# First layer's queries, keys and values in three passes of two-part weight tiles, the recurrence products spread among them, and a second buffer for the state matrices

## The chip, the core and the metric

The kernel runs on one core of a Trainium2 chip. TensorE (PE) multiplies, VectorE (DVE) and ScalarE (ACT) do the elementwise work, GpSimd (POOL) and SyncE (SP) mostly issue transfers; all share an on-chip memory (SBUF), TensorE writes into PSUM banks, and inputs, outputs and intermediate stores lie in the chip's HBM. The metric is the device time of one execution in microseconds; of several runs the median counts.

## What is computed

One sequence of 256 tokens of width 2048 goes through two layers of attention and then through a block with a state-space mixer and an MLP. All of it is float32. Cut to what the change touches:

```python
def first_block(...):
    c_act = jax.nn.silu(c)
    for l in range(DEPTH):                                   # 2 layers
        mod = c_act @ w_mod[l] + b_mod[l]
        shift, scale, gate = jnp.split(mod, 3, axis=-1)
        h = x * (1.0 + scale[:, None]) + shift[:, None]
        y = diff_attention(h, ...) if l < N_A else forgetting_attention(h, ...)
        x = layer_norm(DN_ALPHA * x + gate[:, None] * y, ln_g[l], ln_b[l])
    return x

def diff_attention(h, w_in, w_out, lq1, lk1, lq2, lk2, subln_g, layer_idx):
    proj = h @ w_in                                          # 2048 x 8192
    q, k, v, g = jnp.split(proj, 4, axis=-1)
    ...
    return (rms_norm(o, subln_g) * (1.0 - lam_init) * silu(g)) @ w_out

def s5_scan(u, lam_bar, b_bar, s0, reverse):                 # second block
    bu = jnp.einsum('btgh,gph->btgp', u, b_bar)
    ...                                                      # s_t = lam_bar * s_(t-1) + bu_t
def s5_mixer(h_ctx, h_lat, ...):                             # both directions
    st_ctx = s5_scan(uc_ctx, lam_bar, b_bar, s0, reverse)    # 256 context tokens
    st_lat = s5_scan(uc_lat, lam_bar, b_bar, s_ctx_final, reverse)
    y_lat = y_lat + jnp.einsum('btgp,ghp->btgh', st_lat, c_mat).real
```

The second block's context half (`ctx_2`, the matrices b, c and the eigenvalues) doesn't depend on the first block.

## The kernel before

**Engines.** Each engine has a program written by hand, and semaphores tie them together: a `wait_ge` for one filled or emptied buffer. Weights come in loads of 1 MB that SP issues in one fixed order into a ring of six slots; the load for a slot waits till what stood in it is used up (`spent`). `tables` walks through the same order and hands out slots and PSUM banks, so every program lists the work in the same sequence: 56 "mods" (one mod is a group of 512 columns of the modulation parameters: four loads, 16 matmuls with the column of c as operand, and before them four small `sel` sums of the mod before), the first layer's 16 projection panels of 512 columns (four loads each, handled in halves 0 to 31: queries are halves 0 to 7, keys 8 to 15, values 16 to 23, gates 24 to 31), the context work of the second block, then the 20 + 4 panels around the second layer, the GLU and the MLP ("steps"). The tables `MOD_AT_*` say after which step of a loop a mod stands.

**Two ways to multiply.** The steps run in three passes: ACT copies a weight tile rounded to fp32r as its high part, DVE subtracts (raw - high) for the low part, in place in the ring slot, and PE adds high x high, high x low and low x high. The first layer's panels run in plain float32 instead, straight from the ring: `dense_T` (128x256 results, queries and keys) and `dense_N` (128x512, values and gates), with `hT`, the turned and modulated x, as the other operand. ACT and DVE copy the result of a half to a staging buffer (three of them in MSB, later four more), and POOL's queue stores it (`proj_out`).

**The stages, in order.** (1) Parameters 0 to 7, x turned (`turn_in`), and the 16 turns of b and c by matmuls with the identity (`to_state`). (2) The loop over 16 chunks of the recurrence's kernel: DVE makes the operand `cl` of a chunk with one `cmul` (six operations of 128x1152, then the corner copies of the chunk's product), POOL copies four corner blocks to BBD and stores `cl` to HBM, and PE does a projection half, at every other chunk a mod, and the product `kk` (16 matmuls from BBD). (3) The broadcast columns for the context (`acol`, made by DVE after the lambda vectors of the first layer, which POOL loads at that place), the rows of ctx turned into tables with 32 small matmuls for each `u` product, through copies of 32 rows and DMAs back into SBUF (`arena<-arena`), among them projection halves 18 to 21 and mods 16, 17. (4) The state matrices: in each of 16 chunks `bl` (DVE's `cmul`, six operations of 128x1024), 16 turns by the identity, ACT's four copies into the one buffer MSB (`vmat`), the product `vc` (32 matmuls of 64x32 from MSB) and a store of MSB to `m_state` in HBM, after which ACT may overwrite MSB; halves 22 to 31 stand before chunks 0 to 9 and mods 18 to 24 after seven of them. (5) SP loads the stored projections p0 to p3, and the differential attention runs in 20 steps with mods 25 to 30 at steps 1, 4, ..., 16. (6) The steps of both layers, the GLU and the MLP, with mods 31 to 50 at steps 0 to 19 and 51 to 55 in the second attention.

**Names in the rows.** `arena` is the big SBUF buffer, in which operands, `hT` and the tables lie; `ring`, `in_lo`, `in_hi`, `hid_lo`, `hid_hi`, `MSB`, `BBD`, `cpad` (the column of c), `mod_rows` are SBUF buffers of their own, `bank` is PSUM, `ident` the identity, `sel` the selector of the sums. L1847 is `mm` and L1850 `tr` on PE, L1192, L1196, L1200 and L1204 are DVE's helpers, L777 and L824 ACT's copy and rounding copy.

## Time and profile before

| | us |
|---|---|
| runs shown (3) | median 3030.43, 3026.02 to 3031.03 |
| the profiled execution | 3018.68 |
| its span from first to last instruction | 3016.9 |
| PE busy in it | 2666.4 (88%) |
| DVE busy | 1406.7 (47%) |
| ACT busy | 1005.5 (33%) |
| POOL busy | 155.2 (5%) |
| moved by DMA | 699.74 MB, 232 GB/s in the mean |

The profile is one execution; its time is 0.39% below the median of the runs. A busy share holds for the whole span, and the stages have different limits, so what one engine waits for is read stage by stage. By stage of the list above the profile stands like this: parameters and x to 126 us, turns of b and c to about 147, the projections with the recurrence products to 474.7, the context's tables to 570, the state matrices to 841, the loads and the first attention to 939. The rows in a section below use a few forms. A row of a timeline begins with its start and its duration in us; "x32" is the count of instructions in it, and what stands in brackets is the time that the engine was idle before it and what ended the wait. In a group of rows the numbers after the bar are busy time, mean ns of one, and idle time before them.

### The profile page before, as it was taken

The page shows a single profiled execution, that of the slowest core. Times are in us where ns is not written, and L with a number is a line of the kernel's source. Part 1 is how long each engine was busy: PE and PEld are TensorE (multiplying, and loading weights), DVE is VectorE, ACT ScalarE, POOL GpSimd, SP SyncE. Part 2 cuts the span into 40 slices and gives each one's busy share as a digit, 9 for nine tenths or more (in the row PEclk, how much of TensorE's full clock was granted, in tenths as well). Part 3 has the DMA queues.
Part 4 walks back from the last instruction along what each step waited for, and adds up shares of the span by engine and source line. Part 5 has one row for each costly group of instructions (what it writes and reads, how often), then busy time and mean ns, then how long its engine had stood idle before and what let it go on. Part 6 is the DMA issues. An engine that isn't in the chain of part 4 may idle for free.

```text
span 3016.9 us, 40552 instructions
## 1 busy us (share of the span) xinstructions
PE 2666.4 (88%) x17321; PEld 2087.0 (69%) x17321; DVE 1406.7 (47%) x2074; ACT 1005.5 (33%) x1569; POOL 155.2 (5%) x239
## 2 busy tenths in 40 slices
PE   3899996999767959989999986788969999999996
PEld 0488863445535758769875766567859899898995
DVE  4445441243535766433333453725455545555554
ACT  0200002111224323333332434724454444344443
POOL 2012341000000000000000001000000000000000
PEclk9799998999778979989997795798989999999998
DMA  9868997678597848867886544994534565656552
GB/s 309 310 230 315 346 380 242 193 271 277 205 362 282 313 170 309 309 238 251 313 317 234 182 153 154 182 252 142 184 120 153 184 195 182 195 182 194 183 188 78
DMA packets 333523, 699.74 MB, mean 232 GB/s; under 512 B 14016, under 2 KB 34976, under 8 KB 326944
## 3 DMA queue, kind: packets, MB, share of 16 engines
q1 hardware_dynamic: 313248, 625.17, 62.5%
q0 software_dynamic: 15216, 65.69, 6.1%
q10 hardware_dynamic: 4880, 6.29, 0.8%
...
HBM read 638.38 MB, written 54.53 MB: 230 GB/s over the span
## 4 chain that ended last, share of the span: by engine, by line
PE 79%; DMA 7%; DVE 7%; ACT 4%; issue 2%; POOL 0%; SPq 0%; ACTq 0%; DVEq 0%; POOLq 0%
PE bank L1847 77%; DMA ring<-in_w_mod 4%; PE bank L1850 2%; DVE arena L1192 2%; DVE arena L1200 1%; DMA arena<-arena 1%; ACT arena L777 1%; DVE ring_lo L1192 1%; ACT L774 1%; DMA ring<-in_a_w_out 1%; DVE LT L1200 0%; DVE y_mlp L1200 0%; DMA sm<-in_a_lam_k 0%; ACT MSB L777 0%; DVE att_lo L1192 0%
## 5 line engine op out<-in xcount | busy, mean ns | idle before, releaser
L1192 DVE TENSOR_TENSOR ring_lo<-ring,w_hi 128x1024 fp32r<-128x1024 f32 x320 | 390.1, 1225 | 421.8 <-ACT w_hi L824 421.1
L824 ACT CAST w_hi<-ring 128x1024 fp32r<-128x1024 f32 x320 | 334.7, 1049 | 459.2 <-PE bank L1847 459.0
L1192 DVE TENSOR_TENSOR ring_lo<-ring,att_w_hi 128x1024 fp32r<-128x1024 f32 x192 | 231.0, 1222 | 313.1 <-ACT att_w_hi L824 312.3
L824 ACT CAST att_w_hi<-ring 128x1024 fp32r<-128x1024 f32 x192 | 197.8, 1050 | 396.8 <-PE bank L1847 132.4
L1847 PE MATMUL bank<-ring,arena 128*128 128x512 f32 (+1 forms) x1024 | 300.5, 445 | 27.3 <-issue 26.2
L1847 PE MATMUL bank<-in_hi,w_hi 128*128 128x256 f32 x1024 | 291.1, 284 | 1.1 <-ACT n L774 1.1
L1847 PE MATMUL bank<-in_lo,w_hi 128*128 128x256 f32 x1024 | 291.0, 284 | 0.0
L1847 PE MATMUL bank<-in_hi,ring_lo 128*128 128x256 f32 x1024 | 290.9, 284 | 0.0
L1847 PE MATMUL bank<-ring,cpad 128*32 128x512 f32 x1792 | 247.1, 688 | 43.4 <-DMA ring<-in_w_mod 43.4
L1847 PEld LDWEIGHTS bank<-ring,arena 128*128 128x128 f32 (+1 forms) x1024 | 154.7, 168 | 162.0 <-issue 159.9
L1850 PE MATMUL bank<-ident,arena 128*128 128x128 f32 (+2 forms) x739 | 109.1, 309 | 154.7 <-ACT arena L777 65.2
L1847 PE MATMUL bank<-arena,ring 128*128 128x256 f32 x1024 | 224.7, 380 | 1.6 <-ACT arena L777 1.6
L1192 DVE TENSOR_TENSOR arena<-arena,LT 128x1152 f32<-128x1152 f32 (+1 forms) x128 | 160.7, 1296 | 132.5 <-PE bank L1850 130.5
L1847 PEld LDWEIGHTS bank<-arena,ring 128*128 128x128 f32 x1024 | 193.4, 190 | 30.1 <-issue 4.3
L1850 PEld LDWEIGHTS bank<-ident,arena 128*128 128x128 f32 (+2 forms) x739 | 91.6, 181 | 173.3 <-issue 78.8
L1847 PE MATMUL bank<-att_w_hi,att_hi 128*128 128x512 f32 x512 | 201.3, 393 | 1.1 <-DVE ring_lo L1192 1.1
L1847 PE MATMUL bank<-ring_lo,att_hi 128*128 128x512 f32 x512 | 199.4, 389 | 0.0
L1847 PE MATMUL bank<-w_hi,hid_hi 128*128 128x512 f32 x512 | 199.3, 389 | 0.0
L1847 PE MATMUL bank<-att_w_hi,att_lo 128*128 128x512 f32 x512 | 199.3, 389 | 0.0
L1847 PE MATMUL bank<-ring_lo,hid_hi 128*128 128x512 f32 x512 | 199.2, 389 | 0.0
L1847 PE MATMUL bank<-w_hi,hid_lo 128*128 128x512 f32 x512 | 199.2, 389 | 0.0
L1847 PEld LDWEIGHTS bank<-in_hi,w_hi 128*128 128x128 f32 x1024 | 197.8, 193 | 1.6 <-ACT n L774 1.5
...
## 6 DMA issues: line engine op xcount, KB each, us to landing
ring<-in_w_mod SPq DMA_DIRECT2D x192, 1024.0 KB, 12.0
...
```

Source lines behind the costliest of these rows:

```text
L774: return a.activation(dst, src, f, **kw).then_inc(*(to or o.up("act")))
L777: return a.copy(dst, src).then_inc(*(to or o.up("act")))
L824: a.copy(whi(h), raw_half(h)).then_inc(*o.up("whi"))
L1192: return v.tensor_tensor(dst, x, y, op).then_inc(*(to or o.up("dve")))
L1200: return v.scalar_tensor_tensor(out=dst, in0=x, scalar=s1, in1=y, op0=o1, op1=o2).then_inc(*(to or o.up("dve")))
L1847: return p.matmul(dst, l_, r_, start=start, stop=stop, skip_group_check=True)
L1850: return p.transpose(dst, src, ident[0:k, 0:k])
```

## The change

It does four things.

**Three passes for twelve panels.** `N_PRE` = 12: queries, keys and values are no longer plain float32. Per tile of 128 rows (192 in all) ACT makes the high part in one of five buffers (`PW`, `NT` = 5; they lie in `in_lo`), DVE the low part in the ring slot (`ring_lo`), and PE does its three products (`pre_tile`); x is turned into a high and a low operand (`hid_lo` and `hid_hi` in the rows) with `split_in`. The gates stay in float32 and need `hT`, which DVE adds up again from both parts behind the last panel.

**The order.** After each of the twelve panels stands a mod (8 to 19). The b and c turns stand in the second panel, two after each of its first eight tiles. The 16 recurrence products are no longer between halves: from tile 36 on `tiles_by` spreads DVE's 96 operand operations among the tiles, and `KK_AFTER` puts PE's product of a chunk two tiles behind its last operation. The corner copies of a chunk come after the operand of the next. One temp in MSB (`ct`) takes the place of two. The b and c loads wait on POOL's queue for the loads of mod 6; the lambda vectors come early; `acol` is made at tile 150.

**The stages after.** Gate halves 24 to 26 stand at u products 0, 3, 6, halves 27 to 31 before chunks 1, 4, 7, 10, 13 of the state matrices, mods 20 to 24 after chunks 0, 3, 6, 9, 12. The broadcasts of the context come after the squares on ACT. In the first attention mods 25 to 28 stand at steps 6, 9, 12, 15; the steps 0 to 19 carry 29 to 48, the second attention 49 to 53, and 54 and 55 stand in the second layer's last four panels. Some bias sums move with them.

**Two state buffers.** `vmat` alternates between MSB and a region of the arena (R4), with a semaphore each. SP loads p1 and p2 after product 14 and the eighth store of the arena's buffer.

```diff
-MOD_AT_U, MOD_AT_BL = {5: 17}, {1: 18, 3: 19, 5: 20, 7: 21, 9: 22, 12: 23, 15: 24}
-MOD_AT_A, MOD_AT_B = {1 + 3 * i: 25 + i for i in range(6)}, {2 + 6 * i: 51 + i for i in range(5)}
-MOD_AT_STEP = {n: 31 + n for n in range(20)}
+MOD_AT_PRE, MOD_AT_BL = {pn: 8 + pn for pn in range(12)}, {0: 20, 3: 21, 6: 22, 9: 23, 12: 24}
+MOD_AT_A, MOD_AT_B = {6 + 3 * i: 25 + i for i in range(4)}, {2 + 6 * i: 49 + i for i in range(5)}
+MOD_AT_STEP = {**{n: 29 + n for n in range(20)}, 21: 54, 23: 55}
+N_PRE, NT = 12, 5
+GATE_AT_U, GATE_AT_BL = {0: 24, 3: 25, 6: 26}, {1: 27, 4: 28, 7: 29, 10: 30, 13: 31}
+GATE_OUT_U, GATE_OUT_BL = {5: 24, 6: 25}, {2: 26, 3: 27, 8: 28, 9: 29, 14: 30, 15: 31}
+TILES_FIRST, TILES_B, TILE_M2A = 24, 36, 150
...
+def tiles_by(part):
+    return TILES_B + -(-(16 * N_PRE - TILES_B) * part // 96)
+KK_AFTER = [min(16 * N_PRE, tiles_by(6 * (ch + 1)) + 2) for ch in range(16)]
...
+        cl_bufs = [(reg(R3, 1152), reg(R3 + 1152, 1152)), (reg(R3 + 2304, 1152), reg(R5, 1152))]
+        ct = MSB[:, 0:1152]
+        lamv = MSB[:, 1152:1664]
...
-        vmat = MSB[:, :].rearrange("p (d r m) -> p d r m", d=8, r=2)
+        vrows = [reg(R4, 2048), MSB[:, :]]
+        vmats = [y.rearrange("p (d r m) -> p d r m", d=8, r=2) for y in vrows]
...
+        PHk, PLk, x_raw = DLk, DHk, kmaj(R3)
+        PW = HL[:, 1152:1152 + 512 * NT]
...
-            sp.wait_ge(S["st2"], 16 * 9)
-            sp.wait_ge(S["st3"], 16 * 2)
+            sp.wait_ge(S["st1"], 16 * 11)
+            sp.wait_ge(S["st2"], 16 * 10)
             sp.wait_ge(S["blm"], 16)
+            sp.wait_ge(*filled("vc", 14))
+            sp.wait_ge(S["ms0"], 16 * 8)
...
+            g.wait_ge(*landed("mod", 6, 3))
             for r_, nm in enumerate(("re", "im")):
-                by_pair(reg(R5 + 2048 * r_, 2048), A[f"s5_b_{nm}_2"][0].rearrange("d g p h -> d g (p h)"), "b")
-                by_pair(reg(R5 + 4096 + 2048 * r_, 2048), A[f"s5_c_{nm}_2"][0].rearrange("d g h p -> d g (h p)"), "c")
-            g.dma_start(SUBG[:, :], A["a_subln_g"].to_broadcast([128, 256])).then_inc(S["sub"], 16)
+                by_pair(reg(R1 + 2048 * r_, 2048), A[f"s5_b_{nm}_2"][0].rearrange("d g p h -> d g (p h)"), "b")
+            for r_, nm in enumerate(("re", "im")):
+                by_pair(reg(R2 + 2048 * r_, 2048), A[f"s5_c_{nm}_2"][0].rearrange("d g h p -> d g (h p)"), "c")
...
+            for i, n in enumerate(("a_lam_q1", "a_lam_k1", "a_lam_q2", "a_lam_k2")):
+                g.dma_start(lamv[:, 128 * i:128 * i + 128], A[n].to_broadcast([128, 128])).then_inc(S["lam"], 16)
...
+                while sent < N_PRE and 16 * sent + 20 < tiles_by(6 * ch + 6):
+                    proj_out(2 * sent)
+                    proj_out(2 * sent + 1)
+                    sent += 1
...
+            def tile(i):
+                if i % 4 == 0:
+                    a.wait_ge(*landed("proj", i // 16, i % 16 // 4))
+                if i >= NT:
+                    a.wait_ge(*tile_done(i - NT))
+                copy(tile_hi(i), tile_raw(i), *o.up("thi"))
...
+            for i in range(16 * N_PRE + NT):
+                if i < 16 * N_PRE:
+                    tile(i)
+                pn, k = divmod(i - NT, 16)
+                if pn == 1 and k < 8:
+                    state(2 * k)
+                    state(2 * k + 1)
+                if pn >= 0 and k == 15:
+                    project(2 * pn)
+                    project(2 * pn + 1)
+                    mod(MOD_AT_PRE[pn])
...
             a.wait_ge(S["ctx"], 16)
-            squares_of(ctxv, MU[0]["hc"][:, 0:2048], 0)
-            project(18)
-            project(19)
-            mod(16)
+            squares_of(ctxv, MSB[:, :], 0)
+            a.wait_ge(S["cl0"], 16 * 16)
+            a.wait_ge(S["cl1"], 16 * 16)
+            bcast("ctx_a", MU[0]["a"])
+            bcast("ctx_b", MU[0]["b"])
...
-                    a.wait_ge(S["ms"], 16 * ch)
-                    a.wait_ge(*filled("vc", ch - 1))
+                if ch > 1:
+                    a.wait_ge(S[f"ms{ch % 2}"], 16 * (ch // 2))
                 for h in range(4):
                     r_, half = h // 2, h % 2
                     a.wait_ge(*filled("bl", ch, h))
-                    copy(vmat[:, 4 * half:4 * half + 4, r_, :],
+                    copy(vmats[ch % 2][:, 4 * half:4 * half + 4, r_, :],
...
+            def tiles(n):
+                for i in range(split["n"], n):
+                    v.wait_ge(S["thi"], i + 1)
+                    tt(tile_lo(i), tile_raw(i), tile_hi(i), SUB, *o.up("tlo"))
+                    if i == TILE_M2A:
+                        mod_bias("m2a")
+                        own()
+                        stt(acol, M("m2x", 16), 1.0, C("npre"), ADD, MUL)
+                        stt(acol2, M("m2", 16), 1.0, C("npre"), ADD, MUL, *o.up("acol"))
+                split["n"] = n
...
+                for part in cmul(cT[:, 0], cT[:, 1], L1v, 9, 8 * ch, *cl_bufs[ch % 2], ct, ct, True, "clm"):
+                    tiles(tiles_by(6 * ch + part))
+                if ch:
+                    corners(ch - 1)
...
+            for q in range(4):
+                tt(quarter(hT, q), quarter(PHk, q), quarter(PLk, q), ADD, *o.up("hraw"))
...
-            def project(hp):
+            def gates(hp):
                 for q in (2 * (hp % 2), 2 * (hp % 2) + 1):
-                    (dense_T if hp < 16 else dense_N)(("proj", hp // 2), hT, q)
+                    p.wait_ge(S["hraw"], q + 1)
+                    dense_N(("proj", hp // 2), hT, q)
+            def pre_tile(pn, k):
+                i = 16 * pn + k
+                if k == 0:
+                    room("proj", pn, 0)
+                    room("proj", pn, 1)
+                if pn == 0 and k % 4 == 0:
+                    p.wait_ge(S["hlo"], k // 4 + 1)
+                p.wait_ge(S["tlo"], i + 1)
+                w_hi, w_lo = tile_hi(i), tile_lo(i)
+                for b in range(2):
+                    if pn < 8:
+                        for cb in (2 * b, 2 * b + 1):
+                            blk = slice(128 * cb, 128 * cb + 128)
+                            dst = bank("proj", pn, b)[:, 256 * (cb % 2):256 * (cb % 2) + 256]
+                            for m, (wx, ax) in enumerate(((w_hi, PHk), (w_hi, PLk), (w_lo, PHk))):
+                                t = mm(dst, wx[:, blk], ax[:, k, :], k == 0 and m == 0 and cb % 2 == 0, k == KT - 1 and m == 2)
+                    else:
+                        blk = slice(128 * b, 128 * b + 128)
+                        for m, (wx, ax) in enumerate(((w_hi, PHk), (w_lo, PHk), (w_hi, PLk))):
+                            t = mm(bank("proj", pn, b)[:, :], ax[:, k, blk], wx, k == 0 and m == 0, k == KT - 1 and m == 2)
+                    if k == 15:
+                        t.then_inc(*fill("proj", pn, b))
+                if k < 15:
+                    t.then_inc(S["tile"], 1)
...
+            for pn in range(N_PRE):
+                for k in range(16):
+                    pre_tile(pn, k)
+                    if pn == 1 and k < 8:
+                        state(2 * k)
+                        state(2 * k + 1)
+                    for ch in range(16):
+                        if KK_AFTER[ch] == 16 * pn + k + 1:
+                            corners(ch)
+                mod(MOD_AT_PRE[pn])
...
-            project(19)
-            mod(16)
...
-                if pc in (3, 7):
-                    project(20 + pc // 4)
-                if pc in MOD_AT_U:
-                    mod(MOD_AT_U[pc])
+                if pc in GATE_AT_U:
+                    gates(GATE_AT_U[pc])
...
             for ch in range(17):
-                if ch < 10:
-                    project(22 + ch)
+                if ch in GATE_AT_BL:
+                    gates(GATE_AT_BL[ch])
```

What stands in a row on PE, in the first layer's projections, before (L1847; `arena,BBD` is a recurrence product, `arena,ring` a float32 half, `sel` and `cpad` a mod):

```order
L1847 MATMUL bank<-arena,BBD 32x128 x16
L1847 MATMUL bank<-arena,ring 128x256 x32
L1847 MATMUL bank<-arena,BBD 32x128 x16
L1847 MATMUL bank<-arena,ring 128x256 x32
L1847 MATMUL bank<-sel,mod_rows 128x2 x4
L1847 MATMUL bank<-ring,cpad 32x512 x16
```

and after, at the end of the fifth panel (`mm` is now at L1929, `hid_lo,in_lo`, `hid_hi,in_lo` and `hid_lo,ring_lo` are the three passes of one block of a tile):

```order
L1929 MATMUL bank<-hid_lo,in_lo 128x256
L1929 MATMUL bank<-hid_hi,in_lo 128x256
L1929 MATMUL bank<-hid_lo,ring_lo 128x256
L1929 MATMUL bank<-arena,BBD 32x128 x16
L1929 MATMUL bank<-sel,mod_rows 128x2 x4
L1929 MATMUL bank<-ring,cpad 32x512 x16
L1929 MATMUL bank<-hid_lo,in_lo 128x256
L1929 MATMUL bank<-hid_hi,in_lo 128x256
```

A product stood between two halves of a panel; now it stands behind a tile, here the last one of a panel and ahead of the mod, elsewhere in its midst.

On DVE in the same stage, one chunk before (L1192, two inputs; L1204, the corner copy):

```order
L1192 TENSOR_TENSOR arena<-arena,LT 128x1152 x2
L1192 TENSOR_TENSOR arena<-arena 128x1152
L1192 TENSOR_TENSOR arena<-arena,LT 128x1152 x2
L1200 SCALAR_TENSOR_TENSOR arena<-arena 128x1152
L1204 COPY arena<-bank 128x2x112
L1192 TENSOR_TENSOR arena<-arena,bank 128x2x16
```

and after, one chunk's operand with its tiles (the helpers are 46 lines further down; `ring_lo<-ring,in_lo` is the low part of a tile, `MSB` the shared temp):

```order
L1238 TENSOR_TENSOR arena<-arena,LT 128x1152
L1238 TENSOR_TENSOR ring_lo<-ring,in_lo 128x512 x2
L1238 TENSOR_TENSOR MSB<-arena,LT 128x1152
L1238 TENSOR_TENSOR ring_lo<-ring,in_lo 128x512
L1238 TENSOR_TENSOR arena<-arena,MSB 128x1152
L1238 TENSOR_TENSOR ring_lo<-ring,in_lo 128x512 x2
L1238 TENSOR_TENSOR arena<-arena,LT 128x1152
L1238 TENSOR_TENSOR ring_lo<-ring,in_lo 128x512
L1238 TENSOR_TENSOR MSB<-arena,LT 128x1152
L1238 TENSOR_TENSOR ring_lo<-ring,in_lo 128x512 x2
L1246 SCALAR_TENSOR_TENSOR arena<-arena,MSB 128x1152
L1238 TENSOR_TENSOR ring_lo<-ring,in_lo 128x512 x2
```

Six operations stood in a row; now one or two low parts follow each of them.

On PE between the state matrices, before (`ring,arena` is a half of a gate or value panel, `arena,MSB` the product with a state matrix, `ident,arena` the turns of the next):

```order
L1847 MATMUL bank<-arena,MSB 64x32 x32
L1850 MATMUL bank<-ident,arena 128x128 x16
L1847 MATMUL bank<-sel,mod_rows 128x1 x4
L1847 MATMUL bank<-ring,cpad 32x512 x16
L1847 MATMUL bank<-ring,arena 128x512 x16
L1847 MATMUL bank<-arena,MSB 64x32 x32
L1850 MATMUL bank<-ident,arena 128x128 x16
```

and after (`arena` alone, 64x32, is the product with the matrix in the second buffer):

```order
L1929 MATMUL bank<-sel,mod_rows 128x1 x4
L1929 MATMUL bank<-ring,cpad 32x512 x16
L1929 MATMUL bank<-ring,arena 128x512 x16
L1929 MATMUL bank<-arena,MSB 64x32 x32
L1932 MATMUL bank<-ident,arena 128x128 x16
L1929 MATMUL bank<-arena 64x32 x32
L1932 MATMUL bank<-ident,arena 128x128 x16
L1929 MATMUL bank<-arena,MSB 64x32 x32
L1932 MATMUL bank<-ident,arena 128x128 x16
```

A half stood ahead of each of the first ten products; now it stands ahead of every third, with the mod before it, and the turns and products between stand alone.

## Rows read from the trace of the kernel before

**Rows 1.** Stretches: window, length, busy time of each engine, clock, DMA, GB/s
```profile
0.00:126.00 126.00, 69.73 (x328) 20.42 (x329) 52.87 (x241) 6.31 (x11) 15.77 (x35) 0.79 1.03 340
148.00:450.00 302.00, 301.76 (x1915) 234.91 (x1915) 143.71 (x133) 15.33 (x26) 92.09 (x140) 1.00 0.89 315
773.00:841.00 68.00, 45.68 (x567) 34.46 (x566) 42.76 (x37) 21.80 (x40) 3.22 (x6) 0.74 0.56 206
859.00:939.00 80.00, 66.22 (x376) 35.36 (x376) 37.84 (x113) 31.90 (x116) 0.00 (x0) 0.84 1.04 382
1697.00:1796.00 99.00, 98.54 (x485) 83.35 (x484) 52.87 (x58) 37.47 (x42) 0.53 (x1) 1.00 0.59 198
2268.00:2992.00 724.00, 723.16 (x4640) 662.84 (x4640) 367.87 (x344) 307.28 (x330) 0.00 (x0) 1.00 0.56 178
```

**Rows 2.** Groups of instructions by line and shape: query and key panels
```profile
L1847 PE MATMUL bank<-arena,ring 128*128 128x256 f32 x1024 | 224.7, 380 | 1.6 <-ACT arena L777 1.6
```

**Rows 3.** Timeline: turns and a split; then groups in 126 to 500
```profile
131.97 14.72 PE L1847 MATMUL bank<-ident,arena 128*64 128x128 f32 x256
...
1095.41 4.31 PE L1850 MATMUL bank<-ident,arena 128*128 128x128 f32 x20 [24.39 <-DVE arena L1200]
...
1109.56 1.23 DVE L1192 TENSOR_TENSOR att_lo<-arena,att_hi 128x1024 fp32r<-128x1024 f32 x1 [1.17 <-ACT att_hi L777]
...
L1192 DVE TENSOR_TENSOR arena<-arena,LT 128x1152 f32<-128x1152 f32 x64 | 85.3, 1373 | 2.0
...
L705 POOL COPY BBD<-arena 64x128 f32<-64x128 f32 x64 | 34.6, 570 | 54.2 <-PE bank L1847 53.0
```

**Rows 4.** Timeline, 448 to 511: the last recurrence product and the context's tables
```profile
448.71 1.11 PE L1847 MATMUL bank<-arena,BBD 128*32 128x128 f32 x32
...
472.52 0.49 DVE L1192 TENSOR_TENSOR sm<-sm 128x128 f32<-128x128 f32 x2 [22.02 <-DMA sm<-in_a_lam_k]
474.69 5.51 PE L1847 MATMUL bank<-ident,st 128*128 128x128 f32 x32 [8.67 <-DVE st L1200]
...
492.59 0.88 DVE L1200 SCALAR_TENSOR_TENSOR arena<-arena,st 128x256 f32<-128x256 f32 x2
...
501.25 2.63 ACTq L957 DMA_DIRECT2D arena<-arena  x4
...
510.57 1.04 ACT L777 COPY arena<-arena 32x1024 f32<-32x1024 f32 x1 [8.74 <-DMA arena<-arena]
```

**Rows 5.** Timeline, PE: the turns for the last u product
```profile
568.92 1.18 PE L1850 MATMUL bank<-ident,arena 32*128 32x32 f32 x16
```

**Rows 6.** Timeline, 628 to 842: between the state matrices
```profile
628.43 13.90 PE L1847 MATMUL bank<-ring,arena 128*128 128x512 f32 x32
...
639.56 0.69 DVE L1192 TENSOR_TENSOR arena<-arena,SUBG 128x512 f32<-128x512 f32 x1 [3.78 <-ACT arena L774]
...
642.26 2.06 PE L1847 MATMUL bank<-arena,MSB 128*64 128x32 f32 x64
...
774.13 2.36 DVE L1192 TENSOR_TENSOR arena<-arena,LT 128x1024 f32<-128x1024 f32 x2 [2.98 <-PE bank L1850]
...
783.92 2.36 DVE L1192 TENSOR_TENSOR arena<-arena,LT 128x1024 f32<-128x1024 f32 x2 [2.65 <-PE bank L1850]
...
793.39 1.08 ACT L777 COPY MSB<-bank 128x512 f32<-128x512 f32 x2 [5.67 <-DMA m_state<-MSB]
...
837.35 3.84 PE L1850 MATMUL bank<-ident,arena 128*128 128x128 f32 x16 [4.51 <-DVE arena L1192]
```

**Rows 7.** Timeline, PE, in the first attention: a mod, and the steps around
```profile
893.84 0.95 PE L1847 MATMUL bank<-sel,mod_rows 128*128 128x1 f32 x8
894.72 3.64 PE L1847 MATMUL bank<-ring,cpad 128*32 128x512 f32 x32
...
905.53 0.95 PE L1847 MATMUL bank<-sel,mod_rows 128*128 128x1 f32 x8
```

**Rows 8.** DMA of 148 to 450: GB/s in 40 slices of 7.55 us
```profile
GB/s 0 139 150 190 332 182 101 315 354 391 353 254 302 396 388 174 311 379 386 339 210 272 386 391 229 315 343 396 394 391 347 400 394 395 381 345 396 395 391 382
```

334 lines of the change are left out of this document (156 added, 178 removed).

## The prediction

> **What bounds the kernel now.** I read the stages first [rows 1]: each row is one stretch, with the busy time of each engine, TensorE's granted clock and the DMA share. TensorE (PE) is busy 302 of 302 us in the stretch that projects queries and keys beside the recurrence products (148 to 450), and 723 of 724 in the MLP. So work taken off PE there is time, if its new suppliers keep up. It is not the bound in the last state matrices, 773 to 841 (46 of 68), nor in the attention, 859 to 939 (66 of 80). The timelines say who is waited for: a late load of the lambda vectors and a round trip of small copies in the stage between [rows 4], VectorE (DVE) between the state matrices [rows 6]. The change touches all stages up to 939 and adds to one at 1697; the rest has the same instructions.
>
> **The three-pass stage.** Gone are twelve float32 panels. The eight query and key panels are the x1024 row: 224.7 us, 28.1 each [rows 2]; of a value or gate panel one half takes 13.9 [rows 6]. A panel in three passes of split operands is what the MLP does 32 times in 724 us: 22.6 us [rows 1], so a tile of 128 rows costs 1.41.
>
> First what delays the start. The b and c loads leave the first microseconds and go behind the seventh parameter load. Their 4.2 MB are 12 us of DMA at the 340 GB/s of this stretch [rows 1], so the first loads come that much sooner; but the eighth now runs beside them and must be there before anything starts. I book nothing for it (between -8 and +5). PE turns x from 126, where the first stretch ends [rows 1], and b and c from 132 [rows 3]. Tile 0 then needs the split operand: for the q panel the last low part starts 14.2 us after the turn (1095.4 to 1109.6) and takes 1.2 [rows 3], then one tile of DVE: 16. Start at 142.
>
> Then PE has 12 panels x 22.6 = 271.2; 12 parameter products (mods) of 3.64 + 0.95 = 4.6, together 55.1 [rows 7]; 16 recurrence products at 1.11, 17.8 [rows 4]; and the 16 turns of b and c, 14.7 [rows 3]. That is 359. With 4 for the seams PE stands at the ctx broadcast at 142 + 363 = 505, against 474.7 [rows 4]: **+30**, with 2.5 panels and 3 mods more behind it than before (12 panels for 9.5, mods 8 to 19 for 8 to 15, and one that followed soon after).
>
> Can the suppliers keep up? Between two recurrence products lie (192 - 36)/16 = 9.75 tiles. PE needs 9.75 x 1.41 + 1.1 + 2.8 (its share of mods) = 17.7 us. DVE needs six products of 1.36, 9.75 tiles at 0.69 (a 128x512 tensor_tensor) and 0.6 for the two small corner operations (under half of such a 0.69 each): 8.2 + 6.7 + 0.6 = 15.5 us [rows 3, 6]. ScalarE (ACT) makes the high part of each tile and little else, and I take it to be below DVE; the five tile buffers are 7 us of lead. Inside a pass DVE makes a tile in 1.59 us where PE takes 1.52, losing about 1 us over 16 tiles, and it wins that back in the mod. So it holds, with 2.2 us in 17.7 to spare. DMA: 24 loads of 4.19 MB, 16.8 MB of cl_out, 6.3 of toep, 5.8 of proj and 4.2 of b and c are 134 MB; the last ten slices of this stage before have 345 to 400 GB/s, 383 in the mean [rows 8]: 134/0.383 = 350 us, 9 below PE's 359.
>
> Here a rule speaks against the change. No pair of rows here shows it; POOL's copies are 0.57 us each [rows 3]. The Trainium skill, SBUF — State Buffer, section "SBUF: two separate sides", says that a VectorE op with two SBUF inputs and a GpSimd op that reads SBUF lock each other out of a shared port for the whole instruction. With four such copies a step, 2.3 us, DVE would need 17.8 of 17.7 us, a loss of 0.1 a step and 2 in all.
>
> **The ctx and u stage.** Before, the broadcast column waits for lambda (22.0 us of DVE wait) and the first row copy for project 19 and mod 16: it leaves at 501.25 and lands at 510.57 [rows 4]. Lambda is now loaded early and the column is made at tile 150: neither is waited for. What is late next is ctx itself: its load is issued when DVE has finished the last recurrence operand, some 12 us before the end of the stage, and its 2.1 MB are 6 us at 340 GB/s, twice that in company. Then two squares, the tables and eight broadcast copies: before, the product with the last table began at 492.59 and took 0.88, 18.8 us after the broadcasts began at 474.69 [rows 4]. I take 18.5 from the stage's end to the first row copy, and 9.3 from there to its landing. PE fills with gate half 24 (14.0, the 13.9 and a seam), then u 0 to 2, half 25, u 3 to 5, half 26, u 6 and 7. Before, from the first row copy to the last u took 501.25 to 570.1 = 69 us with two halves and a mod [rows 5]; now no mod, and half 24 is over before u 0 can start: 60. Together 78 for 95.4: **-17** (between -24 and -10).
>
> **The state matrices.** Before, 570.1 to 841.0 = 271 us: ten chunks with a gate half, a product and a turn (14.0 + 2.06 + 2.6 [rows 6], every other one a mod), then six that go at DVE's pace. Now five chunks are mod, half, product, turn: 4.6 + 14.0 + 2.06 + 2.6 = 23.3, together 116.5. The other ten go as the one from 774.13 to 783.92 did: 9.8 us, of which DVE waits 2.65 for PE's turn; where that turn took 3.84, at the end, it is 7.15 + 3.84 = 11.0 [rows 6]. The granted clock was 0.74 in the like stretch [rows 1], so I take 10.4 each. With the first one, 9.7, it is 230: **-41** (between -46 and -30). The second MSB buffer alone is small: ACT waited 5.67 us once for the write out of it [rows 6]. But it keeps the chunks at DVE's pace where no gate half stands between.
>
> **Attention.** SyncE (SP) now waits for the last m_state write into the buffer where p1 lands, about 4 us later than before; the first query product needs p0 and p1. Before, 18 us passed from the end of the last turn, 841, to it at 859, two of the bounds of the stretches [rows 1]; I take 19: **+1** (0 to 4). Then four mods for six, the first at the seventh step instead of the second. Three steps with a mod are 11.7 us (893.84 to 905.53), so a step without its mod is (11.7 - 4.6)/3 = 2.4 [rows 7]. Twenty steps, four mods and 5 for start and end are 72 for 80, and the first mod's loads have six steps to come in: **-8** (between -12 and -3). **Later**, two mods stand in the last four panels of layer 2, where PE is busy 98.5 of 99 us [rows 1]: 2 x 4.6 = **+9**, with nothing to hide them. The moved bias sums are 0.2 us each.
>
> **Sum:** 30 - 17 - 41 + 1 - 8 + 9 = -26 us. The profiled execution took 3018.7 (span 3016.9), so 2992.7. The median of the runs shown is 3030.4, 0.39% higher; less 26 it is **3004**.
>
> **The rule for float32.** The rows give 22.6 for 28.1, a ratio of 0.80. The Trainium skill, FP8 and Floating Point Precision, section "TensorE Precision Notes", has true float32 as four passes, high and low parts against each other; three of four would be 21.1 us a panel, 18 us less over twelve. The rows decide.
>
> **Rivals.** (1) *VectorE becomes the bound* of the three-pass stage: this is the way to slower. For it: 88% busy by my own sum, in strict order, with waits for ACT before each tile and for PE and DMA around each product. Against it: 7 us of lead, and no gaps between its ops in the rows. It decides from 2.2 us a step; each us beyond is 16 us in all. With 3 us more beyond that point the stage takes 48 more: +22, so **3052**. (2) *The loads are the bound.* At the 340 GB/s of the first 126 us [rows 1], 134 MB take 394 us, 35 more than PE's sum; less what overlaps the start, +30: **3034**, no change. For it: 0.97 of what DMA can give, and six slots only. Against it: 390 and more in the late slices. The Trainium skill, DMA: Bandwidth & Descriptors, section "Specifications", gives about 358 GB/s for a core's HBM; 134/0.358 is 374, 15 over PE's sum: 3019. The trace has 383 over ten slices [rows 8] and does not agree. (3) *The idle stretches give more*: u stage 60 us, chunks 9.8, the start 8 sooner: -26 - 10 - 6 = **2988** to 2985. (4) *It does not do what it says*: the tile-wise waits (one for each 1.41 us, not one for 2.8 as in the MLP) break the three-pass rate, 0.1 us a tile: 192 x 0.1 = +19: **3023**.
>
> **How the numbers follow.** Forecast (2993 to 3016) 0.50; more gain (3) 0.16; some stalls, (4) and half of (2), 3016 to 3024, 0.12; (2) 0.10; (1) 0.12. 8 in 10 reach from 2985 to 3033, leaving out the tail below and (1). A measurement here tells about 0.2%, 6 us, from no change: faster 0.78, same 0.10, slower 0.12.
>
> **What would show it.** After: PE at the broadcasts at 505 +- 10 with DVE near 88% in the stretch before; few PE waits for DVE ring_lo there (many, at 1 to 3 us each, is rival 1; ACT waiting for DMA ring<-in_a_w_in is rival 2); lambda nowhere in the chain; u ended 78 us later; chunks at 9.8 to 10.8 with no wait for m_state; first mod of the attention unstalled; the last four panels of layer 2 at 108 us for 98. A stage end beyond 530 makes the forecast wrong, whatever the rest does.

## The result, and the profile after

The changed kernel takes 3048.07 us in the median of four runs (3041.96 to 3052.09), beside 3030.06 for the kernel before on the same chip: a ratio of 1.006, with a 95% interval of 1.0041 to 1.0079. It is slower, by 18 us, and outside the range of the forecast (3004, 2985 to 3033). The profiled execution took 3041.96 (span 3040.2), 23.3 more than the profiled one of before.

The first view is again the one by stages, with the columns of [rows 1]. The first row below stands against the second there, the second against 773 to 841, the third against the attention, the last against the last four panels of layer 2.

```profile
148.00:450.00 302.00, 293.67 (x2631) 253.41 (x2633) 214.04 (x260) 117.92 (x196) 71.65 (x102) 0.99 0.89 317
622.00:855.00 233.00, 186.81 (x1540) 117.31 (x1540) 110.64 (x99) 52.54 (x97) 10.76 (x20) 0.79 0.49 181
884.00:950.00 66.00, 52.75 (x296) 30.65 (x296) 37.75 (x113) 30.83 (x114) 0.00 (x0) 0.91 1.00 363
1707.00:1806.00 99.00, 98.50 (x488) 79.25 (x490) 51.29 (x55) 33.00 (x35) 0.53 (x1) 1.00 0.69 238
```

PE now waits in the projections (294 of 302), and between the state matrices it is busy 187 of 233 us at a mean clock of 0.79. To see where time came and went, the same places are found in both timelines, and only their shifts are compared:

| place | before | after | shift | forecast |
|---|---|---|---|---|
| first broadcast of the context | 474.7 | 528.0 | +53.3 | +30 |
| end of the last u product's turns | 570.1 | 611.2 | +41.1 | +13 |
| end of the last state matrix's turns | 841.2 | 862.4 | +21.2 | -28 |
| first query product of the attention | 858.9 | 883.8 | +24.9 | -27 |
| first step of layer 1's output panels | 963.2 | 975.3 | +12.0 | -35 |
| end of layer 2's output panels | 1788.1 | 1807.7 | +19.6 | -26 |
| end | 3016.9 | 3040.2 | +23.3 | -26 |

Two stages make 44 of the miss of 49 us: the three-pass stage (23 us longer than forecast) and the state matrices (21). Places at which two kernels have run the same program so far differ by up to 3.4 us between their profiles (the last u product, below), so a smaller difference tells little by itself.

**The three-pass stage.** Timeline rows of PE: the first product, one after the clock has risen, then the matmuls of mods 8, 9 and 10, one behind each panel.

```profile
140.38 0.55 PE L1929 MATMUL bank<-hid_lo,in_lo 128*128 128x256 f32 x1 [5.27 <-DVE ring_lo L1238]
...
141.16 0.41 PE L1929 MATMUL bank<-hid_lo,in_lo 128*128 128x256 f32 x1
...
166.22 3.64 PE L1929 MATMUL bank<-ring,cpad 128*32 128x512 f32 x32
...
213.08 3.64 PE L1929 MATMUL bank<-ring,cpad 128*32 128x512 f32 x32
...
241.91 3.64 PE L1929 MATMUL bank<-ring,cpad 128*32 128x512 f32 x32
```

It begins at 140.4 (forecast 142). From 213.08 to 241.91 are 28.8 us, with one recurrence product of 1.1: a panel with its mod takes 27.7 undisturbed, where 27.2 were booked. So the price of three passes was right to 0.5 us. From mod 9 to mod 19 (524.39), ten panels with ten mods and 16 products, 311.3 us went by, and the booked terms make 289.8. The missing 21.5 are 5 of seams (0.5 a panel), 13.2 of waits, and a remainder of 3.3, which the rows put down to slower matmuls behind three of the waits: from 248.9 to 252 us a 128x256 matmul took 0.41 us instead of 0.28, and from 437.0 to 439.5 and from 498.1 to 501.1 a 128x512 one took 0.63 instead of 0.39. Counted up they are 3 to 4 us. The waits, from 213 to 528 us (in all, times, longest):

```profile
PE bank L1929 <- DVE ring_lo L1238: 10.3, 8, 3.1
PE bank L1929 <- DMA ring<-in_w_mod: 2.9, 2, 1.6
...
ACT in_lo L815 <- DMA ring<-in_a_w_in: 119.8, 20, 16.7
```

PE waits for VectorE's low parts, VectorE for ScalarE's high parts, and ScalarE for the loads. One such place, around the start of panel 9:

```profile
422.42 4.47 POOL L736 DMA_DIRECT2D toep<-arena  x6
422.94 3.63 SPq L593 DMA_DIRECT2D ring<-in_a_w_in  x3
424.51 2.18 ACT L815 CAST in_lo<-ring 128x512 fp32r<-128x512 f32 x4 [7.74 <-DMA ring<-in_a_w_in]
426.62 10.98 SPq L593 DMA_DIRECT2D ring<-in_w_mod  x3
435.63 0.62 ACT L815 CAST in_lo<-ring 128x512 fp32r<-128x512 f32 x1 [8.94 <-DMA ring<-in_a_w_in]
437.03 0.80 PE L1929 MATMUL bank<-in_lo,hid_lo 128*128 128x512 f32 x1 [2.82 <-DVE ring_lo L1238]
```

Three of the panel's four loads are issued together when the mod ahead of it frees their slots, beside stores of toep; the next tile reaches ScalarE 12.7 us after that, and PE has by then done what it had of the panel and waited.

**The context.** PE's row at the broadcasts. Half 24 stands behind them and could not fill the wait:

```profile
527.97 2.05 PE L1929 MATMUL bank<-ident,st 128*128 128x128 f32 x16
543.42 3.79 PE L1929 MATMUL bank<-ident,st 128*128 128x128 f32 x16 [13.40 <-ACT arena L815]
```

ScalarE in turn waited for ctx in this stretch (528 to 545 us), and its first row copy left here:

```profile
ACT MSB L812 <- DMA arena<-in_ctx: 7.0, 1, 7.0
554.35 2.92 ACTq L1012 DMA_DIRECT2D arena<-arena  x4
```

The ctx load was issued at 520.9, 7 us before the end of the stage where 12 were forecast, and took 14.9 us. So the first row copy left 26.4 us after the stage's end instead of 18.5. From there to the last u product's turns it took 56.8 us instead of 60, and the stage 83 instead of 78.

**The state matrices.** A period of three chunks on PE (turns, then mod and half together, product, turns, and two chunks without a half):

```profile
667.17 3.81 PE L1932 MATMUL bank<-ident,arena 128*128 128x128 f32 x16 [3.06 <-DVE arena L1238]
670.78 1.71 PE L1929 MATMUL bank<-sel,mod_rows 128*128 128x1 f32 x8
672.41 5.12 PE L1929 MATMUL bank<-ring,cpad 128*32 128x512 f32 x32
677.47 14.00 PE L1929 MATMUL bank<-ring,arena 128*128 128x512 f32 x32
691.40 2.06 PE L1929 MATMUL bank<-arena,MSB 128*64 128x32 f32 x64
693.39 0.66 PE L1932 MATMUL bank<-ident,arena 128*128 128x128 f32 x4
...
703.93 3.82 PE L1932 MATMUL bank<-ident,arena 128*128 128x128 f32 x16 [4.63 <-DVE arena L1238]
708.43 3.62 PE L1929 MATMUL bank<-arena,MSB 128*64 128x32 f32 x64 [0.68 <-ACT MSB L815]
715.12 3.81 PE L1932 MATMUL bank<-ident,arena 128*128 128x128 f32 x16 [3.07 <-DVE arena L1238]
```

The period is 715.12 - 667.17 = 47.95 us, and 44.1 was forecast (23.3 + 2 x 10.4). The part with mod and half, 667.17 to 693.39, took 26.2 us for 23.3, the two chunks without a half 10.5 and 11.2 for 10.4 each. The mod takes 6.7 us instead of 4.6, the turns 3.8 instead of 2.7 and a product 3.6 instead of 2.06: they run at the lower clock level, which was granted after PE had idled in the chunks without a half. Over five such periods that is 19 us, 14.5 of them in the parts with the mod.

### The profile page after: what moved, and what is told of

Read it like the earlier page. It is cut to its first block, busy times and chain, and to the rows that moved or that the text cites. A ratio compares the mean times of both kernels' runs of the same rounds, so it can differ in the third digit from the quotient of the medians.

```text
span 3040.2 us, 42300 instructions
## 1 busy us (share of the span) xinstructions
PE 2642.3 (87%) x17961; PEld 2126.6 (70%) x17961; DVE 1536.8 (51%) x2274; ACT 1121.0 (37%) x1765; POOL 164.4 (5%) x239
## 4 chain that ended last, share of the span: by engine, by line
PE 73%; DVE 11%; DMA 9%; ACT 4%; issue 2%; SPq 1%; ACTq 0%; DVEq 0%; POOL 0%
PE bank L1929 71%; DVE arena L1238 4%; DMA ring<-in_w_mod 3%; PE bank L1932 3%; DMA ring<-in_a_w_in 2%; DVE ring_lo L1238 2%; DVE arena L1246 2%; ACT L812 1%; DMA arena<-proj 1%; DVE LT L1246 1%; DMA ring<-in_a_w_out 1%; ACT arena L815 0%; DMA arena<-in_ctx 0%; DMA arena<-arena 0%; SPq L685 0%
## 5 line engine op out<-in xcount | busy, mean ns | idle before, releaser
L1929 PE MATMUL bank<-in_hi,w_hi 128*128 128x256 f32 x1024 | 291.1, 284 | 2.2 <-issue 2.2
L1929 PE MATMUL bank<-in_lo,w_hi 128*128 128x256 f32 x1024 | 290.9, 284 | 0.0
L1929 PE MATMUL bank<-in_hi,ring_lo 128*128 128x256 f32 x1024 | 290.8, 284 | 0.0
L1929 PE MATMUL bank<-ring,cpad 128*32 128x512 f32 x1792 | 243.1, 680 | 44.1 <-DMA ring<-in_w_mod 41.4
L1932 PE MATMUL bank<-ident,arena 128*128 128x128 f32 (+2 forms) x739 | 121.0, 335 | 161.6 <-DVE arena L1238 49.2
L1932 PEld LDWEIGHTS bank<-ident,arena 128*128 128x128 f32 (+2 forms) x739 | 101.3, 194 | 179.9 <-issue 59.2
L815 ACT COPY arena<-bank 128x512 f32<-128x512 f32 (+2 forms) x200 | 113.5, 619 | 278.0 <-PE bank L1929 211.7
L1929 PE MATMUL bank<-ring,arena 128*64 128x128 f32 (+1 forms) x768 | 190.5, 399 | 26.6 <-issue 26.4
L1929 PE MATMUL bank<-att_w_hi,att_hi 128*128 128x512 f32 x512 | 201.6, 394 | 1.7 <-DVE ring_lo L1238 1.7
L1929 PEld LDWEIGHTS bank<-in_hi,w_hi 128*128 128x128 f32 x1024 | 197.8, 193 | 2.7 <-issue 2.6
L815 ACT CAST in_lo<-ring 128x512 fp32r<-128x512 f32 x192 | 114.5, 622 | 230.7 <-DMA ring<-in_a_w_in 135.7
L1929 PE MATMUL bank<-ring_lo,att_hi 128*128 128x512 f32 x512 | 199.4, 389 | 0.0
L1929 PE MATMUL bank<-w_hi,hid_hi 128*128 128x512 f32 x512 | 199.3, 389 | 0.0
L1929 PE MATMUL bank<-att_w_hi,att_lo 128*128 128x512 f32 x512 | 199.3, 389 | 0.0
L1929 PE MATMUL bank<-ring_lo,hid_hi 128*128 128x512 f32 x512 | 199.2, 389 | 0.0
L1929 PE MATMUL bank<-w_hi,hid_lo 128*128 128x512 f32 x512 | 199.2, 389 | 0.0
L1929 PEld LDWEIGHTS bank<-in_lo,w_hi 128*128 128x128 f32 x1024 | 197.8, 193 | 0.1
L1929 PEld LDWEIGHTS bank<-in_hi,ring_lo 128*128 128x128 f32 x1024 | 197.8, 193 | 0.0
## 6 DMA issues: line engine op xcount, KB each, us to landing
ring<-in_w_mod SPq DMA_DIRECT2D x192, 1024.0 KB, 11.2
```

The lines of the kernel that those rows point to most:

```text
L815: return a.copy(dst, src).then_inc(*(to or o.up("act")))
L1929: return p.matmul(dst, l_, r_, start=start, stop=stop, skip_group_check=True)
L1932: return p.transpose(dst, src, ident[0:k, 0:k])
```

## The experiments

Ratios are to the kernel before on the same chip, with their 95% intervals; times in a stage are from the profiles. The changed kernel stands at 1.006.

**Is it the bytes?** Half of each mod's rows is not loaded in the three-pass stage (PE multiplies the other half twice, so the parameters are not the reference's).

```diff
+                if key[0] == "mod" and 8 <= key[1] < 20:
+                    src = W[k0 + 512 * q:k0 + 512 * q + 256, n0:n0 + 512]...
-                        t = mm(..., w[:, i, :], q == 0, q == 3)
+                        t = mm(..., w[:, i % 2 if 8 <= j < 20 else i, :], q == 0, q == 3)
```

> The changed kernel, but each load of the twelve mods in the three-pass stage (8 to 19) brings half of its rows, and PE multiplies those twice: 25 MB of that stage's 125 MB are left out, and nothing else moves. Theory (loads are the bound late in the stage): the waits of PE for the low parts and for mod loads after 213 us, 14 us in all, and the clock losses behind them go, and PE stands at the context's broadcasts at 505 to 510 instead of 528.0; the whole is 18 to 23 us shorter than the changed kernel's. Rival (VectorE's strict order, the tile-wise waits or the port shared with GpSimd): the waits stay, 525 to 528, and nothing is gained.

The ratio is 1.0012 (0.9995 to 1.0030), some 15 us less than the changed kernel. The stage ends at 515.4, 12.6 earlier, and PE's waits after 213 us fall from 13.2 to 6.1. So loads cause more than half of the 23 us that this stage was longer than forecast; the end was forecast 5 to 10 us too early, since the seams stay.

**Is it VectorE?** 30 more operations of 0.69 us are given to it in the same stage.

```diff
                     tt(tile_lo(i), tile_raw(i), tile_hi(i), SUB, *o.up("tlo"))
+                    if i > 40 and i % 5 == 0:
+                        own()
+                        tt(GXB, PHk[:, 0:2, :]..., PHk[:, 2:4, :]..., SUB)
```

> The changed kernel with one more VectorE operation of 128x512 behind every fifth tile from 45 on, into a spare buffer: 30 of 0.69 us, 21 us more work for VectorE in the stage, 1.35 us in each step between two recurrence products. Theory (VectorE has 2.2 us of 17.7 to spare in a step, and waits for loads besides): within 3 us of the changed kernel. Rival (VectorE sets the stage's pace, and the waits for loads are only seen on ScalarE): 15 to 21 us more.

1.0068 (1.0047 to 1.0089): within 3 us of the changed kernel, though the stage ended 5.9 us later (533.9). 21 us of added work cost 6 there: VectorE is close to the pace but does not set it.

**Is it the six slots?** The same bytes in another order: each mod in four quarters, one behind every fourth tile, so that no four loads are wanted at once.

```diff
+            if k % 4 == 3 and pn in MOD_AT_PRE:
+                ring.use(("mod", MOD_AT_PRE[pn], k // 4), slots)
...
+                    if k % 4 == 3 and pn in MOD_AT_PRE:
+                        mod(MOD_AT_PRE[pn], k // 4)
```

> The changed kernel with each of mods 8 to 19 cut in its four quarters, one behind every fourth tile of its panel, in the loads' order and in PE's; the same bytes, the same products. Theory (the ring's six slots: while a mod stands in one piece behind a panel, its four slots come free at once, the next panel's later loads are issued only then and have some 10 us to land, where 9 to 13 are needed beside the stores): PE's waits after 213 us, 14 us, and the clock losses behind them go, PE stands at the context's broadcasts at 508 to 514 instead of 528.0, and the whole is 14 to 20 us shorter than the changed kernel's. Rival (the bytes alone: 125 MB at what DMA gives): the end of the stage stays at 524 to 528.

Half of the theory held. DMA moved more early (207 GB/s from 180 to 220 us, where the changed kernel has 166), and PE's waits after 213 us fell from 13.2 to 3.4:

```profile
PE bank L1936 <- DVE ring_lo L1245: 2.6, 1, 2.6
PE bank L1936 <- DVE MODC L1245: 0.8, 1, 0.8
```

The stage's end came forward by 8.4 us (519.6), which the rival, the bytes alone, excluded; but not by 14 to 20, and the whole gained nothing that can be told: 1.0057 (1.0039 to 1.0074). The reason is the next wait. The ctx load is issued behind VectorE's last recurrence operand, and PE's wait at the broadcasts grew from 13.4 to 17.6 us:

```profile
PE bank L1936 <- ACT arena L821: 17.6, 1, 17.6
```

At the end of the last u product 4.2 us were left of the 8.4, at the first step 3.2, and at the end of the span none; what is left there is no more than two profiles differ by.

**Is it the place of the ctx load?** The operands are spread over tiles 36 to 176.

```diff
-    return TILES_B + -(-(16 * N_PRE - TILES_B) * part // 96)
+    return TILES_B + -(-(176 - TILES_B) * part // 96)
```

> The changed kernel with the recurrence operands spread over tiles 36 to 176 instead of 36 to 192, so that the last operand, and with it the load of ctx, comes some 24 us earlier. Theory (what PE waits 13.4 us for at the broadcasts is the ctx load, 14.9 us from its issue, with its squares): that wait falls to 3 or less, the last u product ends 72 to 75 us after the stage instead of 83, and the whole is 8 to 12 us shorter than the changed kernel's. Rival (VectorE: 8.75 tiles between products leave it 14.8 us of work in PE's 16): PE's waits for low parts rise by as much, and nothing is gained.

1.0050 (1.0030 to 1.0070). The load left at 488.9 instead of 520.9, PE's wait at the broadcasts fell to 6.5, and from the stage's end to the last u product it took 74 us instead of 83; but the stage ended at 532.2, 4.2 later, with 19.1 us of waits for low parts where the changed kernel had 11.1 in the same window. Nearly half of them are one wait:

```profile
500.76 2.18 ACT L815 CAST in_lo<-ring 128x512 fp32r<-128x512 f32 x4 [17.66 <-DMA ring<-in_a_w_in]
501.41 2.50 DVE L1238 TENSOR_TENSOR ring_lo<-ring,in_lo 128x512 fp32r<-128x512 f32 x4 [13.44 <-ACT in_lo L815]
502.25 0.76 PE L1930 MATMUL bank<-in_lo,hid_lo 128*128 128x512 f32 x1 [8.65 <-DVE ring_lo L1238]
```

VectorE idled there itself, for ScalarE, and ScalarE for a load of the last panel; at the same place of the changed kernel PE waits 3.1 us. So the rival was right that PE would wait more, but 5.5 of the 8 us are a late load and not VectorE's denser work. Whether the ctx load, issued at 488.9 beside the last panel's, made it late, no run shows. The shorter way through the context and the later end of the stage nearly cancel.

**Half 24 ahead of the broadcasts**, as the forecast had assumed it to run:

```diff
+            gates(GATE_FIRST)
             p.wait_ge(S["acol"], 1)
             bcast("ctx_a", acol)
```

> The changed kernel with gate half 24 ahead of the context's broadcasts on PE, and halves 25 and 26 at u products 0 and 3 (nothing at 6). Theory (PE's 13.4 us wait at the broadcasts was left empty because the half stands behind them): from the first broadcast's place to the last u product it takes 68 to 70 us instead of 83, 14 us less in the whole. Rival (the row copies set the u products anyway): at most 3 us less.

1.0065 (1.0042 to 1.0089): nothing to be told. PE idled 4.9 us ahead of the half and took 16.95 us for it instead of 14.0. It ended at 547.6, so the broadcasts came later than ctx wanted them (543.4 in the changed kernel); the first step came 5.4 us earlier by the profile.

**The gaps between the state matrices.** Mods 20 to 24 move by one chunk each.

```diff
-..., {0: 20, 3: 21, 6: 22, 9: 23, 12: 24}
+..., {1: 20, 4: 21, 7: 22, 10: 23, 13: 24}
```

> The changed kernel with one table moved by one: mods 20 to 24 stand behind the turns of chunks 1, 4, 7, 10, 13 instead of 0, 3, 6, 9, 12, so that no gate half follows them and VectorE makes the next operand beside them. Theory (PE idles there for VectorE, and at the lower clock, while mod and half together stand where only 7.2 us of VectorE's work are to be covered): three chunks take 39.5 to 41 us instead of 47.9, and the whole is 32 to 42 us shorter than the changed kernel's 3048, about 3010. Rival (the mod delays the product and with it the copies that VectorE waits for next, so that it only changes place): three chunks take 46 to 48, and nothing is gained.

0.9953 (0.9934 to 0.9972): 32 us less than the changed kernel by the ratios, from one table. Three chunks take 40.6 us (656.90 to 697.50), and the mean clock of the stretch is 0.89 (616 to 824) instead of 0.79. The theory held: an idle gap holds the mod, and the clock falls less.

**Both**, quarters and gaps:

> Both at once: mods 8 to 19 in quarters, and mods 20 to 24 in the gaps between the state matrices (chunks 1, 4, 7, 10, 13). Theory: the two gains lie in different stages and add, 46 to 52 us less than the changed kernel, a ratio to the kernel before of 0.989 to 0.991. Rival (the time saved in one stage is given back in a later one, where loads or VectorE then are late): 0.994 or more, with the missing time as a wait behind 860 us.

0.9962 (0.9948 to 0.9977): no sum. Beside the kernel with the gaps alone the broadcasts come 8.8 us earlier (519.3 for 528.1), but PE waits there 18.2 us for 12.4, and the last u product's turns end at 607.6 for 607.8. So the gain of the quarters is gone before the state matrices begin, not behind 860 us as the rival had it. (Up to that place the kernel with the gaps alone is the changed kernel, which has 611.2 there: the 3.4 us are the difference between two profiles.)

**Mods out of the stage.** The first eight panels keep one in quarters; ten stand in the gaps, one ahead of the attention's loads, and none in layer 2's last four panels.

```diff
+MOD_AT_PRE, MOD_AT_BL, MOD_LAST = {pn: 8 + pn for pn in range(8)}, dict(zip((1, 2, 4, 5, 7, 8, 10, 11, 13, 14), range(16, 26))), 26
+MOD_AT_A, MOD_AT_B = {6 + 3 * i: 27 + i for i in range(4)}, {2 + 6 * i: 51 + i for i in range(5)}
+MOD_AT_STEP = {n: 31 + n for n in range(20)}
```

> As the kernel of both, and mods taken out of the three-pass stage: only its first eight panels have one, ten stand in all the gaps without a gate half (16 to 25), one stands where PE waits for the attention's loads, and none in the last four panels of layer 2. Theory (a mod in a stretch where PE waits for VectorE or for a load costs little, in one where PE is busy 4.6 us): 18 us less for four mods out of the stage, 10 less for the two late ones, and 0 to 10 more for six new ones in the gaps: 18 to 28 us less than the kernel of both, a ratio to the kernel before of 0.980 to 0.984. Rival (ten mods and five halves are 52 MB in some 200 us with the stores of the matrices, and the loads are late there): no less than 0.988.

0.9809 (0.9778 to 0.9841), 46 us less than with both, about twice the 18 to 28 expected. The stage ends at 493.3, 26 us earlier for the 18 of the four mods, and PE waits for nothing in it; and the state matrices, which were to become up to 10 us longer with five mods more, became 10 shorter: from the last u product to the last product 211 instead of 220. The stretches of the two kernels in the middle of that stage, five mods first, ten mods second:

```profile
618.00:815.00 197.00, 165.94 (x1548) 102.30 (x1546) 109.40 (x98) 52.18 (x97) 10.72 (x20) 0.91 0.59 211
```
```profile
590.00:780.00 190.00, 174.08 (x1663) 101.95 (x1665) 109.40 (x98) 53.38 (x100) 10.72 (x20) 0.97 0.90 332
```

The clock is 0.97 with ten. A gap of the second kernel on PE, and the gate half behind it:

```profile
621.32 3.64 PE L1939 MATMUL bank<-ring,cpad 128*32 128x512 f32 x32
624.89 2.06 PE L1939 MATMUL bank<-arena 128*64 128x32 f32 x64
627.96 1.09 PE L1942 MATMUL bank<-ident,arena 128*128 128x128 f32 x8 [1.02 <-DVE arena L1248]
629.36 1.14 PE L1942 MATMUL bank<-ident,arena 128*128 128x128 f32 x8 [0.30 <-ACT MSB L823]
630.34 13.90 PE L1939 MATMUL bank<-ring,arena 128*128 128x512 f32 x32
```

PE waits 1.02 us for VectorE where the changed kernel's gap had 4.63, and every duration is that of the full clock.

**Half 24 first, once more**, in this kernel:

> The same, with gate half 24 ahead of the context's broadcasts and 25 and 26 at u products 0 and 3. In the changed kernel alone this edit brought the attention's steps forward by 5 us and the whole by nothing that could be told. Theory (PE is ready sooner at the last panel here, so half 24 ends before ctx has landed): 8 to 14 us less than the kernel without it. Rival (the broadcasts still wait behind the half, and the row copies set the products): within 5 us of it.

0.9777 (0.9741 to 0.9812). The first step came 5.3 us earlier, the whole 10 by the ratios, with intervals that overlap: between the two theories.

**And the early spread:**

> The best kernel so far (quarters, mods moved out, gaps, half first) with the same spread to tile 176. Theory: ctx has landed when the last panel ends, and 8 to 14 us go, a ratio to the kernel before of 0.973 to 0.975. Rival (in its panels 8 to 11, which have no mod, VectorE was busy 39 of 40 us already, so a denser spread makes PE wait there): a ratio of 0.977 to 0.980.

0.9762 (0.9727 to 0.9798), a median of 2949.76: the best kernel of this study, 2.4% faster than the kernel before. The added gain is 5 us by the ratios, between the two theories and not told from none; the profile has the first query product 2.9 us earlier.

**The second buffer**, undone in the changed kernel and in the best one:

```diff
-        vrows = [reg(R4, 2048), MSB[:, :]]
+        vrows = [MSB[:, :], MSB[:, :]]
...
+                if ch:
+                    a.wait_ge(S[f"ms{(ch - 1) % 2}"], 16 * ((ch + 1) // 2))
+                    a.wait_ge(*filled("vc", ch - 1))
```

> The changed kernel with one buffer for the state matrices as before (each chunk's copies wait for the store of the chunk before and for its product). Theory: only the chunks without a gate half feel it, ten of them from 11 to 12 or 13 us: 10 to 20 us more. Rival (VectorE sets the pace of them anyway, so that the store is hidden): no change.

1.0070 (1.0045 to 1.0094): no difference to be told, against the theory. At 10.5 to 11.5 us a chunk the store is hidden, and ScalarE waited for no store of m_state in that stretch.

> The best kernel (quarters, mods moved out, gaps, half first, early spread) with one buffer for the state matrices. In the changed kernel one buffer made no difference that could be told, with the gaps at the lower clock and 10.5 to 11.5 us long. Theory (it begins to cost where the chunks are short: with ten mods in the gaps a chunk takes 9.9 us, and the first copy of a chunk must wait for the store of the one before, some 8 us after its last copy): ScalarE waits for m_state in most gaps, the state matrices take 10 to 20 us more, a ratio to the kernel before of 0.980 to 0.983. Rival (VectorE's 7.2 us and PE's mod and product still cover the store): 0.976 as with two.

0.9808 (0.9784 to 0.9832), 14 us more than with two, as expected. From the last u product to the last product it takes 219.8 us for 210.5. ScalarE's waits for the store, 575 to 785 us, which the kernel with two buffers has not, are four in all and not in most gaps:

```profile
ACT MSB L825 <- DMA m_state<-MSB: 7.9, 4, 2.5
```

**What the three passes are worth.** The twelve panels go back to plain float32, in the order of the changed kernel and in that of the best.

```diff
-                copy(tile_hi(i), tile_raw(i), *o.up("thi"))
-                    tt(tile_lo(i), tile_raw(i), tile_hi(i), SUB, *o.up("tlo"))
...
+                            t = mm(dst, w[:, blk], hT[:, k, :], k == 0 and cb % 2 == 0, k == KT - 1)
```

> The changed kernel's order with the twelve panels in plain float32: no high and low parts, each tile straight from its ring slot, hT made at the start. Theory (the three passes take 27.7 us for a panel with its mod where float32 takes 32.9, but late loads give a third of it back): 12 x 5.2 = 62 us more of PE's time, less the 18 us of waits and clock losses that vanish because the slower panels leave the loads time: the stage ends at 568 to 574 instead of 528.0, and the whole is 38 to 46 us longer than the changed kernel's, a ratio to the kernel before of 1.018 to 1.022. Rival (the three passes gain nothing here, the tile-wise waits eat it): within 10 us of the changed kernel.

1.0202 (1.0176 to 1.0228): 43 us more than the changed kernel, and the broadcasts at 571.5, both as expected. PE's waits, 145 to 575 us:

```profile
PE bank L1926 <- DMA ring<-in_w_mod: 4.2, 2, 3.7
PE bank L1926 <- DMA ring<-in_a_w_in: 1.0, 1, 1.0
```

> The best kernel's order (quarters, mods moved out, gaps, half first, early spread) with the twelve panels in plain float32. Theory (there the loads are in time, so the whole gain of the three passes is lost): 55 to 62 us more, a ratio to the kernel before of 0.994 to 0.997. Rival (loads still set the end of its stage): 40 us more at most.

0.9961 (0.9949 to 0.9974): 60 us more than the best kernel, 56.8 of them at the broadcasts (568.1 against 511.3). PE waits for nothing in that stage. So of the 62 us that the rows promise the three passes give 60 where the loads are in time, and 43 in the changed kernel's order. Seen the other way, the changed kernel's order with float32 panels is 2.0% slower than the kernel before, 61 us: what the change lost, it lost by its order.

## Why the prediction was wrong

It was wrong in sign: faster was given 0.78, and the kernel is 18 us slower. By its steps:

- **The price of the three passes** was right: 27.7 us for a panel with its mod for 27.2, and the two float32 runs show a gain of 60 and 43 us behind it, where the rows promise 62. The start, 142, was 140.4.
- **"134/0.383 = 350 us, 9 below PE's 359" failed.** It set the stage's mean demand against the mean supply, and the mean was indeed lower: 323 GB/s from 140 to 528 us. But the loads are bound by six slots. While PE does a panel it frees a slot only every 5.6 us, and from 180 to 220 us DMA moved 166 GB/s with nothing to do; behind a mod four slots come free at once, with the stores of that stage on top, from 220 us on. The time that DMA had free early could not be used late: from 470 to 530 us it moved 396 GB/s without a pause. It cost 13.2 us of waits and 3.3 of clock; with half of the mods' bytes gone the stage ended 12.6 earlier, with the quarters 8.4. Rival 2 named the resource and priced it at 30 us, where waits and clock came to 16.5; its chance of 0.10 was too low. Rival 4, a loss of 0.1 us at each tile, came at 0.03 (0.5 us a panel).
- **The seams** were booked at 4 us in all and were 12: 5 in the ten panels, 2.3 in the first (matmuls at the lower clock, 0.41 for 0.28 us, till 146) and 5.0 beside the 14.7 of the b and c turns.
- **The ctx and u stage** gained 12.2 of the 17. "I take 18.5 from the stage's end to the first row copy" was 26.4, since ctx was loaded later and took longer. "PE fills with gate half 24" misread the program: the broadcasts stand ahead of the half on PE, and they wait for ScalarE, which waits for ctx. Moving the half alone or the load alone gained nothing that can be told; both in the kernel with the mods moved out gave 14 us by the ratios (0.9762 for 0.9809), with intervals that overlap.
- **The state matrices, the largest term, failed in both prices.** "4.6 + 14.0 + 2.06 + 2.6 = 23.3" took every part at the full clock, and was 26.2: five times 2.9 us. "The other ten go as the one from 774.13 to 783.92 did", taken at 10.4, was 10.9: ten times 0.5. PE's rows of before say why; the first two are the mod in the gap of that row, the last a mod behind an empty gap:

```profile
773.93 0.95 PE L1847 MATMUL bank<-sel,mod_rows 128*128 128x1 f32 x8
774.81 3.64 PE L1847 MATMUL bank<-ring,cpad 128*32 128x512 f32 x32
...
808.51 5.67 PE L1847 MATMUL bank<-ring,cpad 128*32 128x512 f32 x32
```

  The 9.8 us had a mod in them. It was free there, and PE kept its full clock. I took away this filler, and booked 4.6 us for each mod ahead of a half as well. With the gaps empty the lower clock reaches the turn and the mod behind them, as it had before at 808.51, where a mod took 5.67 us: the turns there cost 1.0 us more and the mod 2.1. I had let the clock of 0.74 raise the price of the gaps and not of what follows them. Five mods moved into gaps gave 32 us back, ten gave more.
- **The second buffer** was told rightly as small here, and the reason given held only where chunks take 9.9 us (in the best kernel): 14 us there, none in the changed kernel.
- **The attention** gained 12.8 for 8; its first query product came 3.6 later for 1. **The late mods** cost 9.8 for 9 in the four panels.
- **Rival 1**, VectorE as the bound, was not it: 21 us more work for it cost 5.9 in the stage and nothing told in the whole. The port rule of the Trainium skill (SBUF — State Buffer, section "SBUF: two separate sides") fits only one side of the pair in the groups of both kernels, 240 to 475 us, before first:

```profile
L1192 DVE TENSOR_TENSOR arena<-arena,LT 128x1152 f32<-128x1152 f32 x48 | 63.9, 1371 | 1.6
...
L705 POOL COPY BBD<-arena 64x128 f32<-64x128 f32 x48 | 27.0, 592 | 36.5 <-PE bank L1847 35.7
```
```profile
L1238 DVE TENSOR_TENSOR arena<-arena,LT 128x1152 f32<-128x1152 f32 x25 | 34.3, 1373 | 1.6
...
L746 POOL COPY BBD<-arena 64x128 f32<-64x128 f32 x52 | 36.0, 720 | 87.9 <-PE bank L1929 87.1
```

  VectorE's operation stays at 1.37 us beside the copies, and GpSimd's copies lengthen from 0.59 to 0.72 (no run here isolates the cause). The 2 us that the rule would have cost VectorE are not there.

What stays open: how the waits and the clock of the three-pass stage divide between bytes and slots (the two experiments overlap), what the seams of 12 us are made of, and why 5 us of the gain in the gaps were given back in the attention (first query product 38.8 us earlier, first step 33.8).
